# The last block's merge gates taken out of its attention and projected during its state space rounds, through DRAM

## The reference, cut to what matters

```python
u = rms_norm_2(h, mix_norm[i])
z = u @ w_in[i]
q, k, v, s_in, gates = jnp.split(z, splits, axis=-1)      # 512, 512, 512, 512, 2048 columns
y_attn = neighbourhood_attention(q, k, v, na_rpb[i]) @ w_attn_out[i]   # 8 heads of 64
y_ssm = s5_branch(s_in, ...) @ w_ssm_out[i]               # 32 groups of 16, two directions
g_attn, g_ssm = jnp.split(jax.nn.sigmoid(gates), 2, axis=-1)
h = h + (g_attn * y_attn + g_ssm * y_ssm) @ w_out[i]
```

## Time and profile before

| | |
|---|---|
| Median of 3 runs | 4028.73 us (4026.52 to 4032.32) |
| The profiled execution | 4037.5 us |
| Its span, first to last instruction | 4035.6 us |
| Busy over the span | PE 3607.2 us (89%), DVE 2361.6 (59%), POOL 2000.9 (50%), ACT 1083.5 (27%) |
| Mean granted clock of PE | 0.940 |
| Weight blocks | 548 of 512 KB, 3.3 us from issue to landing |

### The profile page before, as it was taken

One profiled execution on the slowest core, in us unless ns is written; L12 is line 12 of the kernel. 1 busy time (PEld: TensorE's weight loads), 2 busy tenths in 40 slices (PEclk: granted clock), 3 DMA queues, 4 the chain that ended last, 5 costly groups with the idle time before them and its releaser, 6 DMA issues.

```text
span 4035.6 us, 50468 instructions
## 1 busy us (share of the span) xinstructions
PE 3607.2 (89%) x20020; PEld 3082.5 (76%) x20020; DVE 2361.6 (59%) x3010; ACT 1083.5 (27%) x1832; POOL 2000.9 (50%) x1100
## 2 busy tenths in 40 slices
PE   8899789999999899788899999999845578999998
PEld 7798678899999688666678888888644445778886
DVE  7786789773334866688965333432388833263335
ACT  4306432312211513533132211221125232122201
POOL 4255235466666535333556666666512122556664
PEclk9799899999999989899999999999877789999999
DMA  3122112122223212111222222223211021222232
GB/s 131 43 89 68 36 39 68 68 89 89 88 94 115 79 53 74 48 45 54 74 78 94 94 97 101 94 94 104 81 36 37 21 79 42 73 83 94 94 109 73
DMA packets 86909, 304.86 MB, mean 76 GB/s; under 512 B 9824, under 2 KB 12128, under 8 KB 86752
## 3 DMA queue, kind: packets, MB, share of 16 engines
q1 hardware_dynamic: 80064, 289.44, 21.0%
q10 hardware_dynamic: 6688, 13.32, 0.9%
HBM read 300.62 MB, written 2.10 MB: 75 GB/s over the span
## 4 chain that ended last, share of the span: by engine, by line
PE 66%; DVE 21%; ACT 9%; issue 3%; POOL 0%; DMA 0%; ACTq 0%; DVEq 0%; POOLq 0%
PE acc L431 19%; PE acc L432 19%; PE acc L434 19%; DVE cu L1681 7%; DVE trs L1552 2%; PE aux L577 1%; DVE rh L1642 1%; PE aux L645 1%; PE aux L724 1%; PE aux L660 1%; PE acc L756 1%; DVE zz L1961 1%; PE acc L674 1%; DVE rb L1639 1%; ACT yv L1309 1%
## 5 line engine op out<-in xcount | busy, mean ns | idle before, releaser
L404 POOL TENSOR_SCALAR whi<-raw 128x1024 fp32r<-128x1024 f32 x548 | 610.7, 1114 | 1960.9 <-PE acc L434 1941.6
L406 POOL TENSOR_TENSOR wlo<-raw,whi 128x1024 fp32r<-128x1024 f32 x548 | 1390.2, 2537 | 45.7
L431 PE MATMUL acc<-nhi,whi 128*128 128x512 f32 (+1 forms) x2776 | 960.0, 354 | 52.2 <-DVE mt L1690 26.0
L432 PE MATMUL acc<-nlo,whi 128*128 128x512 f32 (+1 forms) x2776 | 951.7, 351 | 0.0
L434 PE MATMUL acc<-nhi,wlo 128*128 128x512 f32 (+1 forms) x2776 | 872.8, 350 | 0.0
L431 PEld LDWEIGHTS acc<-nhi,whi 128*128 128x128 f32 x2776 | 529.5, 191 | 149.3 <-issue 62.2
L431 PE MATMUL acc<-bhi,whi 128*128 128x264 f32 (+1 forms) x1864 | 564.5, 319 | 27.5 <-ACT rg L1064 12.1
L432 PEld LDWEIGHTS acc<-nlo,whi 128*128 128x128 f32 x2776 | 528.8, 190 | 68.2
L432 PE MATMUL acc<-blo,whi 128*128 128x264 f32 (+1 forms) x1864 | 548.6, 310 | 0.0
L434 PEld LDWEIGHTS acc<-nhi,wlo 128*128 128x128 f32 x2776 | 490.4, 191 | 69.1
L1681 DVE SCALAR_TENSOR_TENSOR cu<-cx,par,cu 128x528 f32<-128x528 f32 (+1 forms) x480 | 485.7, 1066 | 0.0
(11 more groups left out here) (358 smaller groups left out, 4717.2 us busy)
## 6 DMA issues: line engine op xcount, KB each, us to landing
raw<-in_w SPq DMA_DIRECT2D x548, 512.0 KB, 3.3
natab<-in_natab ACTq DMA_DIRECT2D x4, 896.0 KB, 7.3
h<-in_h ACTq DMA_DIRECT2D x8, 264.0 KB, 6.6
rope<-in_rope ACTq DMA_DIRECT2D x2, 1056.0 KB, 6.9
rnn_w<-in_gate ACTq DMA_DIRECT2D x2, 1024.0 KB, 9.8
sbc<-in_ssm ACTq DMA_DIRECT2D x4, 512.0 KB, 3.5
out<-yout SPq DMA_DIRECT2D x8, 256.0 KB, 2.1
pin<-in_p ACTq DMA_DIRECT2D x1, 512.0 KB, 3.9
```

The lines of the kernel that those rows point to most:

```text
L404: pool.tensor_scalar(hi, w, 1.0, 0.0, ALU.mult, ALU.add).then_inc(sem("w_hi"), 1)
L406: pool.tensor_tensor(lo, w, hi.bitcast(F32), ALU.subtract).then_inc(sem("w_split"), 1)
L431: pe.matmul(acc[s][:, f, 0:TH], hi, xh[:, f * TH:(f + 1) * TH], start=a, stop=False)
L432: pe.matmul(acc[s][:, f, 0:TH], hi, xl[:, f * TH:(f + 1) * TH], start=False, stop=False)
```

## The change: what it does, and the diff

- The 16 gate tiles of the second block's merge get phases of their own among the q, k and v tiles of the state space rounds (`QKV_GATES`): three and two in the first round, one and three, one and three, one and two in the others. The blocks of weights are permuted to match.
- After each of them ACT copies the accumulator to one buffer `gout` and issues a transfer of 256 KB to the DRAM tensor `merge_gates`; the next gate's copy waits until that has landed.
- In the attention a head has only its product tile, one part in each of four items. The state space gates are read back by ACT's queue through a ring of four (`sg2`), the first four ahead of the first item; the attention's gates come back in two transfers of 1 MB in the last but one head (`sga`).
- The attention's merge has only its four blocks of products. The sigmoids come from `sga`, and each merged tile is split behind the addition of the next; PE starts `out2` part by part.
- The three zero columns of `rx` are set before the choice of keys, and `top8` moves out of their way.

```diff
--- before.py
+++ after.py
@@ -101,8 +100,13 @@
-ATT_MERGE = [x for i in range(4) for x in ((f"att_gate{2 * i}", 1, 1, 0), (f"att_products{i}", 1, 1, 2),
-                                          (f"att_gate{2 * i + 1}", 1, 1, 1))]
+QKV_GATES = [[("qkv0", "qkv1", "gate0", "gate1", "gate2"), ("qkv2", "gate3", "gate4")],
+             [("qkv3", "qkv4", "gate5"), ("qkv5", "gate6", "gate7", "gate8")],
+             [("qkv6", "qkv7", "gate9"), ("qkv8", "gate10", "gate11", "gate12")],
+             [("qkv9", "qkv10", "gate13"), ("qkv11", "gate14", "gate15")]]
+SSM_TILES = [x for early, late in QKV_GATES for x in (*early, *late)]
+NGATE = 16
+GRING = 4
 PLE = [("ple_gate0", 1, 1, 0), ("ple_products0", 1, 1, 2)] + [(f"ple_gate{i}", 1, 1, i % 2) for i in range(1, 5)] + \
...
@@ -733,18 +750,14 @@
                 def merge_part(j):
-                    i, a, z, end = NA_PARTS[j % NQT]
-                    t = 2 * (j // NQT) + i
+                    t, c = j // NQT, j % NQT
                     s, b = mg.slot(t), mg.block(t)
-                    if a == 0:
+                    if c == 0:
                         pe.wait_ge(evac[s], mg.nth(t))
                         pe.wait_ge(sem("w_split"), b + 1)
-                        if i:
-                            pe.wait_ge(sem("z_lo"), 4)
-                    rhs = R(zhi, zlo, S) if i else R(nhi, nlo, S)
-                    for c in range(a, z):
-                        p = part(s, b % 2, c, rhs, S, c == 0, c == end - 1)
-                    if z == end:
+                        pe.wait_ge(sem("z_lo"), 4)
+                    p = part(s, b % 2, c, R(zhi, zlo, S), S, c == 0, c == NQT - 1)
+                    if c == NQT - 1:
                         p.then_inc(pe_block, 1)
...
@@ -768,11 +781,12 @@
-                qkv = lambda i: tile(AT["qkv2"], i, R(nhi, nlo, S), S)
+                def tiles(names):
+                    for name in names:
+                        tile(AT[name], 0, R(nhi, nlo, S), S)
+
                 for r in range(4):
-                    qkv(3 * r)
-                    qkv(3 * r + 1)
-
+                    tiles(QKV_GATES[r][0])
                     pe.wait_ge(sem("ss_bpow"), 4 * (r + 1))
...
@@ -870,9 +883,9 @@
                 m.then_inc(pe_block, 1)
-                tile(AT[f"att_gate{2 * i + 1}"], 0, R(nhi, nlo, S), S)
-            pe.wait_ge(sem("m2_lo"), KD)
-            with pe.Fori(0, KD // 2) as m:
+            for j in range(2):
+                tile(AT["out2"], j, R(mhi, mlo, S), S, each=("m2_lo", 0) if j == 0 else None)
+            with pe.Fori(1, KD // 2) as m:
                 for j in range(2):
...
@@ -1215,6 +1228,16 @@
+                def fetch(n):
+
+                    if n >= GRING:
+                        act.wait_ge(evac[0], mg.nth(n - GRING) + 1)
+                    act.dma_start(sg2[:, n % GRING], gates[n]).then_inc(sem(f"gate_back{n % GRING}"), 16)
+
+                act.wait_ge(sem("gate_out"), 16 * NGATE)
+                act.wait_ge(sem("z_lo"), 4)
+                for n in range(GRING):
+                    fetch(n)
                 exps(0)
...
@@ -1228,11 +1251,16 @@
                         exps(j + 2)
-                    if i == 2:
-                        t = 2 * hh
-                        block_done(mg.block(t) + 1)
-                        act.wait_ge(evac[0], mg.nth(t))
-                        act.activation(halves(sg2[:, :], S), accv(0, S), ACT.Tanh, scale=0.5).then_inc(evac[0], 1)
+                    if i == 0 and hh + GRING - 1 < HEADS and hh:
+                        fetch(hh + GRING - 1)
+                    if i == 1:
+                        act.wait_ge(sem(f"gate_back{hh % GRING}"), 16 * (hh // GRING + 1))
+                        act.activation(sg2[:, hh % GRING], sg2[:, hh % GRING], ACT.Tanh, scale=0.5).then_inc(sem("gate_tanh"), 1)
+                    if (hh, i) == (HEADS - 2, 0):
+
+                        act.wait_ge(sem("na_scored"), (HEADS - 2) * NQT)
+                        for n in range(0, KD, 4):
+                            act.dma_start(sga[:, n:n + 4], gates[HEADS + n:HEADS + n + 4].rearrange("a p n -> p a n")).then_inc(sem(f"att_gates_back{n // 4}"), 16)
                 act.wait_ge(sem("na_pv"), len(items))
...
@@ -1254,14 +1282,29 @@
             def ssm():
-                qkv = AT["qkv2"]
-
...
-                    dst = (q2, k2, v2)[i // 4][:, i % 4]
-                    block_done(qkv.block(i) + 1)
-                    act.activation(halves(dst, S), accv(qkv.slot(i), S), ACT.Copy, scale=HD2 ** -0.5 if i < 4 else 1.0)\
-                       .then_inc(evac[qkv.slot(i)], 1)
+                    dst, ph = (q2, k2, v2)[i // 4][:, i % 4], AT[f"qkv{i}"]
+                    block_done(ph.b0 + 1)
+                    act.activation(halves(dst, S), accv(ph.slot(0), S), ACT.Copy, scale=HD2 ** -0.5 if i < 4 else 1.0)\
+                       .then_inc(evac[ph.slot(0)], 1)
+
+                def gate(n):
+
+                    ph = AT[f"gate{n}"]
+                    block_done(ph.b0 + 1)
+                    if n:
+                        act.wait_ge(sem("gate_out"), 16 * n)
+                    act.activation(halves(gout[:, :], S), accv(ph.slot(0), S), ACT.Copy).then_inc(evac[ph.slot(0)], 1)
+                    act.wait_ge(evac[ph.slot(0)], ph.nth(0) + 1)
+                    act.dma_start(gates[n], gout[:, :]).then_inc(sem("gate_out"), 16)
+
+                def evacuate(names):
+                    for name in names:
+                        if name.startswith("qkv"):
+                            projected(int(name[3:]))
+                        else:
+                            gate(int(name[4:]))
...
@@ -1280,8 +1323,7 @@
                         repeat_b(0)
-                    projected(3 * r)
-                    projected(3 * r + 1)
+                    evacuate(QKV_GATES[r][0])
                     for g in range(4):
...
@@ -1386,15 +1429,18 @@
             neighbours()
-            for n in range(KD):
-                ph = AT[f"att_gate{n}"]
-                block_done(ph.b0 + 1)
-                if n >= 2:
-                    act.wait_ge(sem("att_product"), n - 1)
-                act.activation(halves(sga[:, n % 2], S), accv(n % 2, S), ACT.Sigmoid).then_inc(evac[n % 2], 1)
-            for n in range(KD):
+
+            def merged_high(n):
                 act.wait_ge(sem("m2_add"), n + 1)
...
+
+            for n in range(KD):
+                act.wait_ge(sem(f"att_gates_back{n // 4}"), 16)
+                act.activation(sga[:, n], sga[:, n], ACT.Sigmoid).then_inc(sem("att_sigmoid"), 1)
+            for n in range(KD):
+                if n:
+                    merged_high(n - 1)
+            merged_high(KD - 1)
             squares(6, AT["out2"])
...
@@ -1602,9 +1648,6 @@
             def rnn(l):
-                dve.wait_ge(sem("ix_relu"), (l + 1) * NQT * IXH)
-                dve.memset(rx[:, 0:CONV - 1], 0.0).then_inc(sem("rnn_pad"), 1)
-                dve.wait_ge(sem("rnn_pad"), l + 1)
                 ph = AT[f"rnn{l}"]
...
@@ -1653,6 +1696,9 @@
                 ph = AT[f"conv{l}"]
+                dve.wait_ge(sem("ix_relu"), (l + 1) * NQT * IXH)
+                dve.memset(rx[:, 0:CONV - 1], 0.0).then_inc(sem("rnn_pad"), 1)
+                dve.wait_ge(sem("rnn_pad"), l + 1)
                 for n in range(KD):
...
@@ -1817,10 +1863,11 @@
                     if i == NQT - 1:
-                        block_done(mg.block(2 * hh + 1) + 1)
-                        then(dve.tensor_scalar(sg2[:, :], sg2[:, :], 0.5, 0.5, ALU.mult, ALU.add))
-                        dve.tensor_tensor(halves(merged2[:, hh], S), accv(0, S), halves(sg2[:, :], S), ALU.mult)\
-                           .then_inc(evac[0], 1)
+                        g = sg2[:, hh % GRING]
+                        dve.wait_ge(sem("gate_tanh"), hh + 1)
+                        then(dve.tensor_scalar(g, g, 0.5, 0.5, ALU.mult, ALU.add))
+                        block_done(mg.block(hh) + 1)
+                        dve.tensor_tensor(halves(merged2[:, hh], S), accv(0, S), halves(g, S), ALU.mult).then_inc(evac[0], 1)
                 part(3)
...
@@ -2033,19 +2080,22 @@
+
+            def merged_low(n):
+                dve.wait_ge(sem("m2_hi"), n + 1)
+                dve.tensor_tensor(mlo[:, n], merged2[:, n], mhi[:, n].bitcast(F32), ALU.subtract).then_inc(sem("m2_lo"), 1)
+
             for n in range(KD):
-                dve.wait_ge(evac[n % 2], AT[f"att_gate{n}"].nth(0) + 1)
+                dve.wait_ge(sem("att_sigmoid"), n + 1)
                 block_done(AT[f"att_products{n // 2}"].b0 + 1)
-                dve.tensor_tensor(mt2[:, :], aux[n % 4 // 2][:, n % 2, :], sga[:, n % 2], ALU.mult)\
+                dve.tensor_tensor(mta[:, :], aux[n % 4 // 2][:, n % 2, :], sga[:, n], ALU.mult)\
                    .then_inc(sem("att_product"), 1)
                 dve.wait_ge(sem("att_product"), n + 1)
-                dve.tensor_tensor(merged2[:, n], merged2[:, n], mt2[:, :], ALU.add).then_inc(sem("m2_add"), 1)
```

(11 more changed lines are left out.)

37 lines of the change are left out of this document (25 added, 12 removed).

## The result

The changed kernel takes 3969.2 us (median, 3962.1 to 3972.5) against 4027.8 beside it: a ratio of 0.9847, 95% interval 0.983 to 0.9863 (55 to 69 us). The medians differ by 58.6 us; the forecast was 75 us, to 3954, in a range of 3917 to 3984. The profiled execution took 3972.5 us, 65.0 less than the one of before.

A forecast was written before the change was run, and what follows sets the result against it. It took DVE to bound the state space rounds, with 130 us of PE to spare, and PE the attention and its merge. Terms -54 - 50.9 + 38.9 - 9 = -75 gave 3962.5 profiled, median 3954 us, range 3917 to 3984.

The forecast's parts named there:

- The likeliest case: The forecast itself: attention -54, merge -50.9, rounds +38.9, zero columns -9, to 3954 us; chance 0.55.
- PE is warmer: Rounds: the output before E (a round's output end) takes 5.5 us, not 7.7, -2.2 in rounds two to four; sums -0.8 each.
- taken by likeness to the others: First round: with three gates there, its sums come some 6.2 us late as well, between 0 and 12.
- The splits in the early part fall in DVE's slack: Rounds, ahead of the sums: POOL's splits of gate weights there cost nothing, as DVE's chain is 38 us against 44.
- The early gate: Rounds two to four: PE starts it at E + 19.8, cold, 8.35 us; sums at E + 41.4, not 35.3: +6.1 a round.
- The splits: Rounds: POOL's weight splits slow DVE's scans (2.0 us) and states (2.86): 4.8, 7.3, 7.3, 4.8 us before the states.
- the two longer items: Attention, each head's first and last item: DVE's chain takes 4.40 and 4.44 us, 0.84 and 0.88 over PE's 3.56.
- the 10 us kept for the slow clock: Attention: matmuls at 1.2 GHz cost nothing to 17 us; 10 kept on top of 130, so 140 in place of 194.4.
- Rounds that hide nearly all: Rival: PE's spare 130 us in the rounds exceed the gates' 89, so rounds +8, total 3923 us; chance 0.13.
- Stretched rounds: Rival: rounds +60 by longer splits, attention only -40 as its PE stays at 1.2 GHz longer, total 3993; chance 0.15.
- The DRAM buffer: Rival: ACT's gate copies wait for the last transfer to land; slower, at 12 us a transfer 4058 us; chance 0.05.
- An item of 5 us: Rival: in the attention a chain of DVE and ACT sets 5 us an item, total 3984 us; chance 0.12.

The follow-up runs named there:

- b_zero: The kernel before, with only the zero columns of `rx` set ahead of the convolution's inputs and `top8` moved out of that place: 4023.1 us, ratio 0.9982.
- no_split: The changed kernel, with POOL splitting only 128x8 of each gate's 128x1024 block of weights: 3940.7 us, ratio 0.9779.
- no_tiles: The changed kernel, with 3 matmuls instead of 24 in each of the 16 gate tiles: 3957.4 us, ratio 0.9814.
- evac_first: The changed kernel, with ACT evacuating the first waiting projection tile ahead of the 32 copies to `us` and the second after 24 of them: 3946.3 us, ratio 0.9793.
- hole: The changed kernel, with one more PE wait per attention head, for that head's tanh before the merge tile's second part: 4005.2 us, ratio 0.9934.
- low_last: The changed kernel, with the merge's eight low parts formed behind all additions and `out2` started when all are there: 3971.9 us, ratio 0.9859.

## Why the prediction was right or wrong

The likeliest case came true in its mechanisms, not in its sizes: the rounds lie at the far end of their bounds and the attention outside its own. That the sum is only 10 us too large in the profiled pair (75 against 65.0; 16 by the medians) is luck, since the two errors nearly cancel.

| Term | Forecast | Profiled pair |
|---|---|---|
| Attention | -54 | -67.4 |
| Merge to `out2`'s first tile | -50.9 | -49.5 |
| Rounds | +38.9 | +60.0 |
| Zero columns | -9 | -9.5 (b_zero alone: -7) |
| Between rounds and attention | 0 | +0.6 |
| Behind `out2`'s first tile | 0 | +0.8 |
| Sum | -75 | -65.0 |

**The rounds, +21 off.** From the first to the last round's states I had written 20 to 30 us more; it was 45.7. By their parts, over four rounds:

- *"PE is warmer: ... I take 5.5, -2.2 in rounds two to four; the sums -0.8 in each"*: the step that failed most, -9.8 forecast, +1.5 measured (outputs +0.9, sums +0.6). PE still pauses 7.1 us ahead of the output and 4.4 ahead of the sums, and a pause of 7.1 left it as slow as one of 16.6: outputs of 7.1 us after, 6.3 to 6.6 before in the later rounds. I had compared with the 7.70 of the first round alone. Only where a tile ended 0.6 us ahead of the output (no_split) did all of it run fast.
- *The first round, "taken by likeness to the others"*, 6.2 ahead of the sums: measured 8.3, from another cause. There the bound is DVE's own chain, and three splits stand beside it:

```profile
2958.32 2.22 DVE L2143 TENSOR_TENSOR cp__143<-cp__143,cs__146 128x1280 f32<-128x1280 f32 x1
2960.58 3.57 DVE L2140 TENSOR_TENSOR cp__143<-sbc,lc_i 128x1280 f32<-128x1280 f32 x1
2964.18 2.22 DVE L2140 TENSOR_TENSOR cs__146<-sbc,lc_r 128x1280 f32<-128x1280 f32 x1
2966.44 3.58 DVE L2146 TENSOR_TENSOR cp__143<-cp__143,cs__146 128x1280 f32<-128x1280 f32 x1
2970.05 1.55 DVE L2148 TENSOR_SCALAR cp__143<-cp__143 128x1280 f32<-128x1280 f32 x1
2971.75 3.13 DVE L1886 TENSOR_TENSOR m<-spw,chk 128x1024 f32<-128x1024 f32 x1 [0.15 <-DVE cp__143 L2148]
```

  Over 1.49, 0.83 and 1.22 us undisturbed they lose 0.73 + 2.08 + 0.73 + 2.09 + 0.72 + 1.91 = 8.26: all of it. "The splits in the early part fall in DVE's slack" was false here. no_tiles gains nothing, and no_split and evac_first bring these sums 4.9 and 5.5 us sooner; in both one split still meets this chain (its loss in no_split: 2.7).
- *The early gate, +6.1*: start E + 19.8, 8.35 us and end E + 28.2 came as worked out. Measured +7.3 to +7.9, since the transposes and lags behind it did not stay warm (`w1s` 1.34, 1.34, then 1.81 apart; lags 4.35 and not 3.6).
- *The splits, 4.8 / 7.3 / 7.3 / 4.8*: measured 5.2 / 8.2 / 8.3 / 5.5. Place and kind right, a tenth too small: ten more splits cost 2.7 each, also those put at 2.0 and 2.5. A split takes 0.7 with its first operation and 2.0 with its subtraction, whether it meets a scan or another operation. In the earlier trace rows too the 0.77 belong to POOL's first operation (3029.37 to 3030.42) and not to the second, as the prediction had it.

**The attention, -13 off.** The item (3.55 measured, 3.56 forecast), the two longer items (4.34 and 4.41 against 4.40 and 4.44) and every second head's 0.6 stood. 130 us were worked out and 127.0 measured; wrong were the 10 us kept for the slow clock. The other 3 lie mainly in the ends of the stage: the last head, without scores to come, takes 11.9 us and the first 18.3, instead of 16.3. hole shows that such a clock comes with waits inside a head, and this change had taken those waits away.

**The merge** came within 1.4 us and **the zero columns** within their bounds; low_last and b_zero each bear one out.

**The rivals.** Rounds that hide nearly all: refuted (60). Stretched rounds did come, at the upper bound I had given, but with a fast attention instead of the slow one that I had tied to them: the two were not one case. The DRAM buffer: transfers landed in a median of 2.6 us, and no gate's copy in the changed kernel waited for one. An item of 5 us: refuted.

The Trainium skill (SBUF — State Buffer, Who interferes with whom) says that VectorE and GpSimd lock each other out for a whole instruction. The traces agree, also that a one-input TENSOR_SCALAR can be caught (0.83 to 1.55, 0.69 to 2.72). The size agrees once POOL's own waiting is taken off: its operations of 1.05 and 2.35 us cost DVE 0.7 and 2.0, each about 0.3 less than its length. So POOL's first operation does hold DVE off, as the prediction drew from this rule; but its loss was already in the 2.86, and a split costs 2.7 us and not up to 3.4.
